# Scored rows read the normed token from PSUM, and key scores are copied out early by ScalarE

## What is computed

```python
def peer(h, w_q, sub_keys, u_tab, v_tab):              # h: 256 tokens x 2048, normed
    q = (h @ w_q).reshape(1, 256, 8, 2, 64)            # 8 heads, two halves
    s = einsum("blhsk,hsnk->blhsn", q, sub_keys)       # 128 key scores per head and half
    s1, i1 = top_k(s[..., 0, :], 16)
    s2, i2 = top_k(s[..., 1, :], 16)
    cand_s = s1[..., :, None] + s2[..., None, :]       # 16 x 16 candidates per head
    top_s, pos = top_k(cand_s, 16)                     # 16 of them: idx in 0..16383
    g = softmax(top_s)
    u = take(u_tab, idx)                               # 128 rows of 2048 per token
    act = gelu(einsum("td,tkd->tk", h, u))
    v = take(v_tab, idx)                               # 128 more rows of 2048 per token
    return einsum("tk,tkd->td", g * act, v)
```

## Time and profile before

| | us |
|---|---|
| median of 3 runs | 3179.36 (3177.67 to 3188.95) |
| profiled execution, its own time | 3179.81 |
| its span, first to last instruction | 3178.5 |
| first gather issued at | 2099.32 |
| last of the u rows is scored by | 3104.6 |
| last matmul of the v rows ends at | 3167.7 |

### The profile page before, as it was taken

How to read it: one execution, slowest core, us unless ns; L and a number is a source line. 1 busy time by engine, 2 the same in 40 slices (tenths; PEclk the granted TensorE clock), 3 DMA queues, 4 the chain that set the end, 5 groups by cost and what they waited for, 6 DMA issues and landing times.

```text
span 3178.5 us, 35017 instructions
## 1 busy us (share of the span) xinstructions
PE 2834.2 (89%) x12772; PEld 1978.6 (62%) x12772; DVE 2251.9 (71%) x3698; ACT 1054.9 (33%) x2125; POOL 1446.2 (45%) x1973
## 2 busy tenths in 40 slices
PE   6999999899999999999998999983888888788887
PEld 4678888556688888787876778771333333333333
DVE  5558887866767776656885555589777877878666
ACT  5454245234355544444514544510101110111101
POOL 6677877750000000000120000048878888788886
PEclk9999999999999999999999999996999999998999
DMA  9977585544647775554554563579999999999997
GB/s 378 387 274 279 205 270 206 212 159 159 197 149 249 238 235 176 194 197 171 186 168 132 185 212 133 192 290 420 413 418 418 418 418 410 392 418 414 397 401 273
DMA packets 297868, 877.50 MB, mean 276 GB/s; under 512 B 28731, under 2 KB 153019, under 8 KB 226491
## 3 DMA queue, kind: packets, MB, share of 16 engines
q1 hardware_dynamic: 216448, 417.56, 37.8%
q0 software_dynamic: 77024, 447.08, 34.8%
q10 hardware_dynamic: 4224, 10.62, 0.9%
HBM read 965.94 MB, written 17.96 MB: 310 GB/s over the span
## 4 chain that ended last, share of the span: by engine, by line
PE 59%; DVE 16%; issue 8%; POOL 7%; DMA 7%; ACT 3%; SPq 0%; ACTq 0%; POOLq 0%; DVEq 0%
PE lin L568 13%; PE lin L493 7%; PE lin L495 6%; PE lin L494 6%; PE lin L570 6%; PE lin L3566 6%; PE lin L394 4%; DMA ring<-in_peer_v,arena 3%; DVE ring L3721 3%; POOL ring L3808 2%; POOL ring L3812 2%; DVE arena L3721 2%; DVE scratch L915 2%; DMA arena<-in_peer_u,arena 2%; DVE weight_parts L451 1%
## 5 line engine op out<-in xcount | busy, mean ns | idle before, releaser
L451 DVE TENSOR_TENSOR weight_parts<-ring,weight_parts 128x512 fp32r<-128x512 f32 (+2 forms) x994 | 672.8, 690 | 464.0 <-ACT weight_parts L439 459.0
L439 ACT CAST weight_parts<-ring 128x512 fp32r<-128x512 f32 (+2 forms) x994 | 593.7, 607 | 697.1 <-PE lin L495 350.2
L568 PE MATMUL lin<-parts,weight_parts 128*128 128x512 f32 x1792 | 641.1, 401 | 12.8 <-DVE weight_parts L451 9.6
L3566 PE MATMUL lin<-ring,scratch 128*128 128x512 f32 x1136 | 539.0, 627 | 109.0 <-DMA ring<-in_peer_v,arena 64.2
L570 PE MATMUL lin<-parts,weight_parts 128*128 128x256 f32 x1792 | 502.6, 280 | 0.0
L3566 PEld LDWEIGHTS lin<-ring,scratch 128*128 128x128 f32 x1136 | 221.5, 200 | 420.6 <-issue 349.2
L3721 DVE CUSTOM_DVE_ANT_0 ring<-ring,arena 128x2048 f32<-128x2048 f32 x168 | 384.3, 2295 | 137.2 <-DMA ring<-in_peer_u,arena 136.1
L493 PE MATMUL lin<-weight_parts,parts 128*128 128x512 f32 (+2 forms) x1092 | 418.9, 384 | 23.5 <-DVE weight_parts L451 15.8
L3808 POOL DMA_INDIRECT ring<-in_peer_u,arena x168 | 276.8, 1648 | 302.3 <-DVE arena L3583 231.0
L494 PE MATMUL lin<-weight_parts,parts 128*128 128x512 f32 (+2 forms) x1092 | 410.1, 376 | 0.0
L495 PE MATMUL lin<-weight_parts,parts 128*128 128x512 f32 (+2 forms) x1092 | 410.0, 375 | 0.0
(11 more groups left out here) (332 smaller groups left out, 3790.5 us busy)
## 6 DMA issues: line engine op xcount, KB each, us to landing
ring<-in_ada_row_loads SPq DMA_DIRECT2D x64, 1024.0 KB, 8.4
ring<-in_w_in_fourier SPq DMA_DIRECT2D x64, 1024.0 KB, 8.5
ring<-in_ada_front_loads SPq DMA_DIRECT2D x32, 1024.0 KB, 8.7
ring<-in_w_in_attn SPq DMA_DIRECT2D x32, 1024.0 KB, 6.6
ring<-in_w_out_fourier SPq DMA_DIRECT2D x16, 2048.0 KB, 7.9
ring<-in_w_in SPq DMA_DIRECT2D x24, 1024.0 KB, 7.5
ring<-in_mem_k_loads SPq DMA_DIRECT2D x16, 1024.0 KB, 9.9
ring<-in_w_out_attn SPq DMA_DIRECT2D x8, 2048.0 KB, 8.0
```

The lines of the kernel that those rows point to most:

```text
L439: c.nc.scalar.copy(c.w_parts[:, q, 0, 0:L.per * w], weights_of(c, L, load, w, k)).then_inc(c.a_high.after(("high", L.name, i)), 1)
L451: c.nc.vector.tensor_tensor(c.w_parts[:, q, 1, 0:L.per * w], weights_of(c, L, load, w, k), c.w_parts[:, q, 0, 0:L.per * w].bitcast(F32), A ...
L568: c.nc.tensor.matmul(pairs(banks[j][:, :]), c.w_parts[:, q, 0, b], x, start=(k == 0), stop=False, skip_group_check=True)
L3566: mm = nc.tensor.matmul(X.sums[t][b][:, :], c.diag[:, X.diag_of(t, k), :], X.buf_of[t, 1, k][:, b * 512:(b + 1) * 512], start=(k == PE_ROW ...
```

## The change

1. Of the 256 scored rows, 220 read the normed token from PSUM in place of SBUF: all from slot 32 on in tile 0 and from slot 4 on in tile 1 (`scores_from_psum`). The token lies in the four `aux` banks, which are now one tensor `aux_all`. ACT copies it there (`a_hn_up`, four copies of 128x512), for tile 0 once all key scores have left the banks, for tile 1 once the last row of tile 0 is scored. The gathered row is still read from SBUF, and the products are still written to SBUF.
2. For the last seven of the eight groups of two heads, PE makes all key scores at the start, and ACT copies them out of PSUM (`a_key_scores`) to seven places of their own: five in `scratch`, one in the place of the first two queries, one in `X.sc`. DVE's copy (line 3615) is left for the first group alone. ACT's copy for the second group stands between its copies of the queries.

```diff
+        self.aux_all = self.ctx.enter_context(nc.psum_tensor("aux", [P, 4 * 512], F32))
+        self.aux = Banks([self.aux_all[:, i * 512:(i + 1) * 512] for i in range(4)])
...
+        self.later = [(t, h) for t in range(NT) for h in range(0, E_HEADS, HH) if (t, h) != (0, 0)]
+        rows = c.scratch[:, 1024:3584].rearrange("p (g q n) -> p g q n", g=5, q=HH * 2)
...
         if h == HH:
             yield from pe_choose(c, X, 0, h)
+    for t, h in X.later[1:]:
+        yield from pe_choose(c, X, t, h)
     for n, (t, table, k) in enumerate(ORDER):
         if table == 0:
-            choice = choice_at(t, k)
-            if choice is not None and choice[2] == 0 and choice[:2] != (0, 1):
-                yield from pe_choose(c, X, choice[0], choice[1] * HH)
             continue
...
+def scores_from_psum(t, k):
+
+    return k >= (2 * TOPK if t == 0 else 4)
+
 def v_scored(c, X, t, k):
     yield from c.v.wait_ge(("got", t, 0, k))
-    buf = X.buf_of[t, 0, k]
+    buf, hn = X.buf_of[t, 0, k], X.hn[:, t, :]
+    if scores_from_psum(t, k):
+        yield from c.v.wait_ge(("hn_up", t))
+        hn = c.aux_all[:, :]
     names = [("scored", t, k // TOPK)] if k % TOPK == TOPK - 1 else []
-    c.nc.vector.tensor_tensor_reduce(out=buf, in0=buf, in1=X.hn[:, t, :], scale=1.0, scalar=0.0, op0=ALU.mult,
+    c.nc.vector.tensor_tensor_reduce(out=buf, in0=buf, in1=hn, scale=1.0, scalar=0.0, op0=ALU.mult,
...
+        if h == HH:
+            yield from a_key_scores(c, X, 0, h)
+    for t, h in X.later[1:]:
+        yield from a_key_scores(c, X, t, h)
+    yield from a_hn_up(c, X, 0, [("free", key) for key in c.aux.holder])
     for n, (t, table, k) in enumerate(ORDER):
         h = k // TOPK
+        if (t, table, k) == (1, 0, 0):
+            yield from a_hn_up(c, X, 1, [("row_used", 0, 0, E_SLOTS - 1)])
...
+def a_key_scores(c, X, t, h0):
+
+    out = X.sc_of[t, h0].rearrange("p (h s) n -> p h s n", s=2)
+    if (t, h0) == X.later[-1]:
+        yield from c.a.wait_ge(("idx", 0, HH - 1))
+    for sd in range(2):
+        key = ("key_scores", t, h0, sd)
+        yield from c.a.wait_ge(("full", key))
+        c.nc.scalar.copy(out[:, :, sd, :], c.bank[key][:, 0:HH * E_KEYS].rearrange("p (a b) -> p a b", a=HH)).then_inc(
...
+def a_hn_up(c, X, t, before):
+
+    yield from c.a.wait_ge(*before)
+    for b in range(4):
+        c.nc.scalar.copy(c.aux_all[:, b * 512:(b + 1) * 512], X.hn[:, t, b * 512:(b + 1) * 512]).then_inc(
+            c.a_step.after(*([("hn_up", t)] if b == 3 else [])), 1)
```

More of the change, by code:

```diff
@@ L170, in __init__ @@
         self.lin = Banks([self.ps(f"lin{i}") for i in range(4)])
-        self.aux = Banks([self.ps(f"aux{i}") for i in range(4)])
+        self.aux_all = self.ctx.enter_context(nc.psum_tensor("aux", [P, 4 * 512], F32))
+        self.aux = Banks([self.aux_all[:, i * 512:(i + 1) * 512] for i in range(4)])
         self.bank = {}
@@ L3398, in __init__ @@
         self.sc = c.at(15 * K1, HH * 2, E_KEYS)
+        self.later = [(t, h) for t in range(NT) for h in range(0, E_HEADS, HH) if (t, h) != (0, 0)]
+        rows = c.scratch[:, 1024:3584].rearrange("p (g q n) -> p g q n", g=5, q=HH * 2)
+        self.sc_of = {key: rows[:, i] for i, key in enumerate(self.later[:4] + self.later[5:6])}
+        self.sc_of[self.later[4]] = self.qT[:, 0:HH, :].rearrange("p h (s n) -> p (h s) n", n=E_KEYS)
+        self.sc_of[self.later[6]] = self.sc
         self.cand = c.at(15 * K1 + 512, HH, TOPK, TOPK)
@@ L3610, in v_choose @@
     ls = slice(2 * h0 * TOPK, 2 * (h0 + n) * TOPK)
[L3611 to L3616, removed]
+    kept = X.sc_of.get((t, h0), X.sc)
+    if (t, h0) in X.sc_of:
+        yield from v.wait_ge(("scores", t, h0))
+    else:
+        sc = kept.rearrange("p (h s) n -> p h s n", s=2)
+        for sd in range(2):
+            key = ("key_scores", t, h0, sd)
+            yield from v.wait_ge(("full", key))
+            nc.vector.tensor_copy(sc[:, 0:n, sd, :], c.bank[key][:, 0:n * E_KEYS].rearrange("p (a b) -> p a b", a=n)).then_inc(
+                step.after(("free", key)), 1)
     yield True
     i1q, v1q = (x.rearrange("p (q k) -> p q k", k=TOPK) for x in (X.i1, X.v1))
-    yield from v_top16(c, lambda q: X.sc[:, q, :], lambda q: v1q[:, 2 * h0 + q, :],
+    yield from v_top16(c, lambda q: kept[:, q, :], lambda q: v1q[:, 2 * h0 + q, :],
                        lambda q: i1q[:, 2 * h0 + q, :], 2 * n)
@@ L3780, in a_experts @@
             yield from a_rstd(c, ("out", t), st_tmp(c, 1))
+def a_key_scores(c, X, t, h0):
+    out = X.sc_of[t, h0].rearrange("p (h s) n -> p h s n", s=2)
+    if (t, h0) == X.later[-1]:
+        yield from c.a.wait_ge(("idx", 0, HH - 1))
+    for sd in range(2):
+        key = ("key_scores", t, h0, sd)
+        yield from c.a.wait_ge(("full", key))
+        c.nc.scalar.copy(out[:, :, sd, :], c.bank[key][:, 0:HH * E_KEYS].rearrange("p (a b) -> p a b", a=HH)).then_inc(
+            c.a_step.after(("free", key), *([("scores", t, h0)] if sd else [])), 1)
+def a_hn_up(c, X, t, before):
[3 more added lines that the diff above has]
+            c.a_step.after(*([("hn_up", t)] if b == 3 else [])), 1)
 def last_load(L):
```

## The result

The changed kernel takes 3168.99 us (median of 8 runs, 3166.77 to 3171.48), the kernel before beside it 3186.28 (8 runs, 3177.67 to 3189.64). The ratio is 0.9947, with a 95% interval from 0.9936 to 0.9959: 17 us faster. The profiled execution took 3169.42 us, its span 3167.8.

What follows compares the result with a forecast made beforehand. Transfers at 418 GB/s were taken to bound the gather stage, with dips from held gathers. From 3179.81 us, 15.0 for dips and 2.8 for the end gave 3162.0, forecast 3162; 8-in-10 range 3154 to 3179.

Steps and rivals of the forecast that it cites:

- the likeliest case: Whole kernel: faster than before by over 0.5%, given a chance of 0.53.
- What bounds the kernel: Gather stage: transfers bound it at 418 GB/s; held gathers keep POOL from refilling a queue that has run low.
- the four slow stretches: Gather stage, 205 us in all at 401, 384, 364 and 392 GB/s; PE and DVE said not to be full.
- Part 1, the hold: 220 scored rows: token in PSUM ends the hold on gathers; a row takes 2.28 us against 2.29, cost nothing.
- 15.0 us of 16.1 for the dips: Gather stage: DMA time back from stretches below 418 GB/s, at most 16.1 us; 15 taken, 1.1 staying after tile 0.
- 2.8 us for the end: After the last scored row: PE's 2.76 us wait for a v row goes, worth between nothing and 2.8 us.
- Part 2 at nothing: Key scores moved from DVE to ACT: no gain by itself, no cost, or 2.4 us if PE's slack is gone.
- The sum and its base: Whole kernel: 3179.81 us profiled, less 15.0 and 2.8, gives 3162.0; run median 0.45 us lower, so 3162.
- The dips stay in part: Rival, dense gather stretches: buffers or uneven DMA engines limit, only about 9 us come back, 3170 us; chance 15%.
- The queue that is always full is faster than 418: Rival, 2220 to 3102 us: 420 GB/s saves another 4.4 us, 3156.5 us with all 16.1 recovered; chance 8%.
- The hold stays: Rival, scored rows: the hold comes from writing products or the instruction itself, not its second input; 3179 us; chance 11%.
- slower: Rival, scored rows: they take longer with the token in PSUM, 3440 us at half the rate; chance 6%.

Runs made afterwards that it cites:

- half_rows: Changed kernel, but of the scored rows moved to PSUM only the even ones read it, the odd ones SBUF: 3167.73 us, ratio 0.9961 to the kernel before.
- pool_one: Changed kernel with one 128x512 write of zeros on GpSimd ahead of each gather: 3171.86 us, ratio 0.9964 to the kernel before.
- paced8: Changed kernel where each gather also waits until the row eight gathers before it is used: 3197.13 us, ratio 1.0039 to the kernel before.
- after_again: The second measurement of the changed kernel, with no edit, beside the kernel before: 3168.13 us, ratio 0.9956.
- scores_alone: Changed kernel with all scored rows reading the token from SBUF again, key scores still set aside by ACT: 3186.30 us, ratio 1.0008 to the kernel before.
- tile0_only: Changed kernel with only the first tile's scored rows (from row 32) reading PSUM, the second tile's SBUF: 3179.19 us, ratio 0.9983 to the kernel before.
- tail_psum: Changed kernel with VectorE's running sum in PSUM over the last 32 added rows of the second tile: 3166.65 us, ratio 0.9936 to the kernel before.

## Why the prediction was right

The forecast was 3162 us with 0.53 for faster by over 0.5%; it came out as 3168.99, 0.53% faster (interval 0.41 to 0.64%), inside the range and in the likeliest case, near the line of 0.5% where the forecast had put itself. On which side of that line the change lies isn't settled: the second measurement has 0.44% (0.31 to 0.57%). The mechanism was right; that the total came so near the forecast is in part luck, as the two terms below show. Point by point:

- **What bounds the kernel.** Right: the transfers at 418 GB/s. The text called POOL's 1.99 us a gather "just the pace of the transfers" and put the loss to a queue that isn't filled again; half_rows, pool_one and paced8 bear this out. One sentence of it misread the rows: PE is full in one of the four slow stretches, 20.00 of 20 us from 2620. It wasn't the bound there, for with PE at 20.00 again the changed kernel has 417 GB/s.
- **Part 1, the hold.** Right, and the row is 2.29 us as before (2286 ns on average, forecast 2280). half_rows shows it side by side. "Whatever its own start" is nearly so: a gather that starts in the row's first 0.04 us isn't held.
- **15.0 us of 16.1 for the dips.** In rates, 14.8: the windows above have the stretches at 418 but for 417 in 20 us (0.05 us) and 415 in 175 (1.3 us). The 1.1 us that I held back for the end of tile 0 was put in the wrong place; that stretch is at 418. The last scored row starts only 11.0 us earlier, though (10.5 in after_again): the term was too large by over a third. A stretch that I hadn't counted, 2646 to 2731, fell from 419 to 416, 0.6 us. Most of the difference is in the windows over the whole stage: 410 GB/s in 1003.02 us before, 416 in 991.99 after, 411 and 413 MB. A fuller queue has carried some 1.4 MB more by then, v rows behind the last u row, which is 3 us at 418 (whole-number rates leave this open by 2).
- **2.8 us for the end.** Measured 5.7, of which the change accounts for 3.6 to 4.0. The wait of 2.76 us is gone, PE runs from 3101.83 to 3157.04 without one, and two later groups take 0.9 us less, delays too short for a row of their own. The 1.7 us of the first 32 matmuls, 14.00 in place of 15.70, are the clock, and after_again, which doesn't have them, is 3.6 us shorter than before. "Every microsecond that the last u row lands earlier moves the end by one" agrees with this. The terms were 15.0 and 2.8, the first profiles show 11.0 and 5.7, 16.7 against 17.8; with after_again's profile it is 10.5 and 3.6, 14.1, which is also what its ratio says (14.0 us).
- **Part 2 at nothing.** Right: scores_alone is at 1.0008. PE's matmuls for key scores ahead of its first v row are 48, 4.07 us, and not 24; they stand where PE then waits 56.31 us for its first diagonal, so they cost nothing.
- **The sum and its base.** 17.8 us off the profiled execution; the medians of the runs differ by 17.3, in the second measurement by 12.9. The absolute figure missed by 7 us because the base did: the three runs shown had a median of 3179.36, eight of the same kernel 3186.28. For a kernel whose bottleneck engine is full to the last per cent, three runs are a poor base.
- **The rivals.** *The dips stay in part* fell: 415 GB/s over 175 us is all that is left of them. *The queue that is always full is faster than 418* fell: the middle of the first tile still ran at 418, and in the second, with gathers landing after 18.4 us (after_again), the rate was 417. *The hold stays* and *slower* fell with half_rows and the 2286 ns. That buffers are POOL's limit in the changed kernel came true (95.9 and 49.9 us of waiting for PE between 2600 and 3090), without costing the rate.
- **Not foreseen.** That POOL, at 2.00 us a gather, stood at the decision point, so that half of the holds could have stayed; and that the dips move between executions, so that the first tile may lose more in others. The forecast read only the dips of one execution.

What stays open: whether a POOL that is as full without holds costs the same; why tile0_only's tail was 68.8 us in its profile (2.9 us are in its first 32 matmuls, at the lower clock, and 5.0 in waits for v rows, which nothing explains); why the clock fell behind the same 3.2 us of idle time in some executions and not in one; and how the gain splits between the tiles closer than 9 and 5 us.

## What to carry to other kernels

When an engine issues transfers for a stage that they bound, add up its time for each issue, pauses included, and set it against the time of one transfer. Clearly under it (here 1.77 against 1.99 us) an interference cost nothing; at it, delays stayed, and the loss showed as holes in the rate at places that change from run to run. Before a difference of 2 us is put down to a change, compare the granted clock of the same stretch. An edit that brings nothing may have uncovered a second bound of the same height: look at which engine is at 20 of 20 us, and try the pair.

## What the runs showed of the hardware

- A VectorE instruction of 2.29 us with two SBUF inputs lengthened an indirect gather's issue from 0.94 to 3.00 us, until 0.81 us behind its own end; with one of the inputs in PSUM, and the output still in SBUF, it didn't.
- Where the accumulator of a `scalar_tensor_tensor` row lies, SBUF or PSUM on both sides, doesn't change its time. Groups of tail_psum, the forms with a running sum in `arena` and in `aux`:

```profile
L3707 DVE SCALAR_TENSOR_TENSOR arena<-ring,arena 128x2048 f32<-128x2048 f32 x18 | 42.3, 2350 | 0.0
L3707 DVE SCALAR_TENSOR_TENSOR aux<-ring,arena,aux 128x2048 f32<-128x2048 f32 x10 | 23.5, 2354 | 5.8 <-DMA ring<-in_peer_v,arena 5.2
```

- More gathers in the queue (18.4 us to landing in after_again against 12.9 in tile0_only) took the mean rate of the second tile from 407 to 417 GB/s, not above the 418 of the best stretches before; they closed its holes.
- After the same 3.2 us of idle time PE's granted clock over its next 4 us was 0.58 and 0.57 in two executions and 1.00 in a third: 32 matmuls of 128x512 took 15.70 us or 14.00.
